# A hierarchical mixture-of-experts trunk on one core: half of the read-back by plain loads, placing matrices by GpSimd, weight rows in pairs, and a reordered passage to the experts

## What is computed

```python
h = rmsnorm(x, norm_ffn)                      # x is (512, 1024)
gl = h @ w_group + b_group                    # 4 groups
el = (h @ w_router + b_router)                # 16 experts, 4 in each group
g_idx = argmax(gl); top_v, top_i = top_k(el of that group, 2)
wts = softmax(top_v) * softmax(gl)[g_idx]
gate = sum over the two of one_hot(g_idx * 4 + top_i) * wts
for e in range(16):                           # EXPERT_FF = 512
    a = silu(h @ w_gate[e]) * (h @ w_up[e])
    out = out + gate[:, e:e + 1] * (a @ w_down[e])
x = x + out
return rmsnorm(x, norm_final)
```

## Time and profile before

| | |
|---|---|
| Median of 3 runs | 730.58 us (729.27 to 730.77) |
| The profiled execution, its own time | 730.31 us |
| Its span in the profile | 728.6 us |
| PE busy | 699.1 us (96%) |
| DVE busy | 518.7 us (71%) |
| ACT busy | 401.8 us (55%) |
| POOL busy | 128.5 us (18%) |
| TensorE clock granted, mean | 0.99 |

### The profile page before, as it was taken

The page is one execution under the profiler, slowest core; times in us unless marked ns, Lnnn a source line. Parts: engine busy times, 40 slices in busy tenths (PEclk is TensorE's granted clock), DMA queues, the critical chain, the costliest instruction groups (busy, mean ns, idle before and its releaser), DMA issues.

```text
span 728.6 us, 9970 instructions
## 1 busy us (share of the span) xinstructions
PE 699.1 (96%) x3557; PEld 582.1 (80%) x3557; DVE 518.7 (71%) x554; ACT 401.8 (55%) x407; POOL 128.5 (18%) x145
## 2 busy tenths in 40 slices
PE   5999999999999999999999989999999999999982
PEld 4898888888888888888889758888888888888861
DVE  4688776898526061441744678999999999999975
ACT  6626665666522131222403336877777777777742
POOL 5320000000000000000000150333333333333132
PEclk9999999999999999999999999999999999999997
DMA  9675330000232233223593379999999999999886
GB/s 327 165 263 180 116 97 20 29 13 4 94 124 80 92 101 121 95 87 113 177 363 126 130 269 393 395 390 369 372 365 379 373 369 371 373 368 372 316 159 188
DMA packets 86753, 159.15 MB, mean 218 GB/s; under 512 B 6274, under 2 KB 37116, under 8 KB 86724
## 3 DMA queue, kind: packets, MB, share of 16 engines
q1 hardware_dynamic: 78544, 137.38, 53.0%
q0 software_dynamic: 8128, 21.37, 9.3%
q10 hardware_dynamic: 52, 0.01, 0.0%
HBM read 150.64 MB, written 15.73 MB: 228 GB/s over the span
## 4 chain that ended last, share of the span: by engine, by line
PE 84%; DVE 5%; DMA 5%; ACT 3%; issue 1%; POOL 1%; POOLq 0%; SPq 0%; DVEq 0%; ACTq 0%
PE ps L519 24%; PE ps L521 24%; PE ps L520 24%; DMA x<-y_rows 3%; PE ps L1614 2%; DVE ring_lo L487 2%; PE ps L1540 1%; DMA xn<-in_x 1%; PE ps L1671 1%; PE ps L1568 1%; PE ps L1398 1%; DVE soft L1935 1%; PE ps L1360 1%; PE ps L1640 1%; ACT ring_hi L481 1%
## 5 line engine op out<-in xcount | busy, mean ns | idle before, releaser
L487 DVE TENSOR_TENSOR ring_lo<-raw_a,ring_hi 128x2048 fp32r<-128x2048 f32 (+2 forms) x58 | 115.5, 1995 | 96.7 <-ACT ring_hi L481 96.7
L487 DVE TENSOR_TENSOR ring_lo<-raw,ring_hi 128x2048 fp32r<-128x2048 f32 x71 | 161.3, 2290 | 11.1 <-ACT ring_hi L481 9.9
L481 ACT ACTIVATE ring_hi<-raw 128x2048 fp32r<-128x2048 f32 x71 | 136.2, 1920 | 19.3 <-PE ps L521 19.3
L481 ACT ACTIVATE ring_hi<-raw_a 128x2048 fp32r<-128x2048 f32 (+2 forms) x58 | 97.4, 1680 | 33.5 <-PE ps L521 30.6
L519 PE MATMUL ps<-hT_hi,ring_hi 128*128 128x512 f32 x288 | 113.4, 394 | 1.6 <-DVE hT_lo L1791 1.0
L521 PE MATMUL ps<-hT_hi,ring_lo 128*128 128x512 f32 x288 | 112.2, 390 | 0.0
L520 PE MATMUL ps<-hT_lo,ring_hi 128*128 128x512 f32 x288 | 112.2, 390 | 0.0
L519 PE MATMUL ps<-ring_hi,xT_hi 128*128 128x512 f32 x240 | 95.0, 396 | 1.8 <-DVE xT_lo L2173 1.7
L521 PE MATMUL ps<-ring_hi,xT_lo 128*128 128x512 f32 x240 | 93.8, 391 | 0.0
L520 PE MATMUL ps<-ring_lo,xT_hi 128*128 128x512 f32 x240 | 93.6, 390 | 0.0
L519 PEld LDWEIGHTS ps<-hT_hi,ring_hi 128*128 128x128 f32 x288 | 54.1, 188 | 13.0 <-DVE ring_lo L1786 1.2
(11 more groups left out here) (369 smaller groups left out, 1241.1 us busy)
## 6 DMA issues: line engine op xcount, KB each, us to landing
raw<-in_w_down SPq DMA_DIRECT2D x25, 1024.0 KB
raw<-in_w_gate SPq DMA_DIRECT2D x47, 512.0 KB
raw<-in_w_up SPq DMA_DIRECT2D x47, 512.0 KB
raw_a<-in_w_in SPq DMA_DIRECT2D x15, 1024.0 KB
raw_a<-in_w_gate SPq DMA_DIRECT2D x17, 512.0 KB
raw_a<-in_w_up SPq DMA_DIRECT2D x17, 512.0 KB
raw_a<-in_w_down SPq DMA_DIRECT2D x7, 1024.0 KB
raw_a<-in_w_in SPq DMA_DIRECT2D x10, 512.0 KB, 8.3
```

The lines of the kernel that those rows point to most:

```text
L481: act.activation(ring_hi[:, c[0] % SPLIT, 0:width], buf[:, 0:width], ACT.Copy).then_inc(hi_ready, 1)
L487: dve.tensor_tensor(ring_lo[:, s, 0:width], buf[:, 0:width], ring_hi[:, s, 0:width].bitcast(F32), ALU.subtract).then_inc(lo_ready, 1)
```

## The change

**Read-back.** The rows with r = 0 are now loaded by SP with four plain DMAs into `y_in`, a view of the first two buffers `raw_a`, when these chunks are split and the stores have landed; DVE adds them to `x2` (`add_rows`). POOL keeps the four adding DMAs with r = 1. DVE's order at the end becomes: low part of tile 14, `add_rows` 0 and 1, low part of tile 15, `add_rows` 2, `add_placed` 0 and 1, `add_rows` 3, `add_placed` 2 and 3.

**Places.** POOL writes `tok` and `place_l` for the last two tiles, behind its last store and ahead of the adding DMAs, once the chunk that lay in `place_l`'s memory is split.

**Pairs.** For experts 1 to 15 a chunk's partition p holds rows 2p and 2p + 1 (one run of 4 KB in HBM, 8 KB for `w_down`) in place of rows p and p + 128. PE's transposes take every second column accordingly (`pair_block`). Expert 0 keeps its loads.

**Passage.** Expert 0's product goes to banks 7 and 4 in place of 0 and 1; ACT alone copies `xT_f` (now in memory of its own) in four signalled pairs, and PE starts on the first pair; `rows_of_slots` moves ahead of block 3 and `x_transpose` of expert 1 ahead of the last block. DVE makes the picks (8 small operations) before the last ranks arrive, does `xT_lo` of expert 1 between the two splits, and the router's weights after the third. ACT splits the third chunk earlier. POOL's first gather takes its indices straight from `x_row`. SP no longer waits for `xe_in[1]`.

```diff
-    xT_f = sb("xT_f", [P, D], F32, "m", 32 * KB)
+    xT_f = sb("xT_f", [P, D], F32, "m", 44 * KB)
+    y_in = raw_a[:, :, :].rearrange("p s (h d) -> p (s h) d", d=D)
+    FIRST_BANK = (7, 4)
...
+            def paired(rows_ap):
+                return rows_ap.rearrange("(p k) n -> p (k n)", k=2).unsqueeze(1)
             def expert_in(c, i, e):
                 k0 = 2 * i * P
-                load(c, [((0, CW // 2, 2), w_gate[0, e, k0:k0 + 2 * P, :].rearrange("(k p) n -> p k n", p=P)),
-                         ((CW // 2, CW, 2), w_up[0, e, k0:k0 + 2 * P, :].rearrange("(k p) n -> p k n", p=P))])
+                load(c, [((0, CW // 2, 1), paired(w_gate[0, e, k0:k0 + 2 * P, :])),
+                         ((CW // 2, CW, 1), paired(w_up[0, e, k0:k0 + 2 * P, :]))])
...
                     if n == 0 and i == 1:
                         sp.wait_ge(route_ready, 1)
-                        sp.wait_ge(xe_in[1], 16)
...
+            sp.wait_ge(lo_ready, split_count(K(C_OVER - 11)))
+            for b in range(2):
+                sp.wait_ge(y_out[b], 16 * (NE // 2 - 1))
+                sp.sem_inc(sp_free, 1)
+            for t in range(TB):
+                sp.dma_start(y_in[:, t, :], rows_of(t, 0)).then_inc(y_load[t // 2], 16)
...
-            x_load(1, 1, None)
+            pool.sem_inc(x_col_set, 1)
+            pool.indirect_dma_start(xe[1][:, :], None, h2_rows[:, :],
+                                    bass.IndirectOffsetOnAxis(x_row[:, 1:2].bitcast(U32), 0),
+                                    bounds_check=S - 1, oob_is_err=False).then_inc(xe_in[1], 16)
...
             y_store(NE - 3, 1, NE // 2 - 1)
+            pool.wait_ge(lo_ready, split_count(K(C_OVER - 5)))
+            for b, tile in ((0, NE - 2), (1, NE - 1)):
+                done(pool.tensor_copy(tok[b][:, 0:1], x_row[:, tile:tile + 1]))
+                for t in range(1, TB):
+                    ins = pool.tensor_scalar(tok[b][:, t:t + 1], tok[b][:, 0:1], float(-P * t), None, ALU.add)
+                done(ins)
+                for t in range(TB):
+                    pool.tensor_scalar(place_l[b][:, t, :], slot_no_f[:, :], tok[b][:, t:t + 1], None,
+                                       ALU.is_equal).then_inc(place_set, 1)
             for b in range(2):
                 pool.wait_ge(y_out[b], 16 * (NE // 2 - 1))
                 pool.sem_inc(pool_free, 1)
-            for r in range(2):
-                for t in range(TB):
-                    if r == 1:
-                        pool.wait_ge(y_back[t], 16)
-                    pool.dma_start(x2[:, t, :], rows_of(t, r), accum_op=ALU.add).then_inc(y_back[t], 16)
+            for t in range(TB):
+                pool.dma_start(x2[:, t, :], rows_of(t, 1), accum_op=ALU.add).then_inc(y_back[t], 16)
...
-            for k in range(4):
-                ins = act.activation(xT_f[:, k * P:(k + 1) * P], bank(2)[:, k * P:(k + 1) * P], ACT.Copy,
+            for k in range(KD):
+                if k == 4:
+                    act.wait_ge(xe_ps, 2)
+                ins = act.activation(xT_f[:, k * P:(k + 1) * P], bank(2 + k // 4)[:, k % 4 * P:(k % 4 + 1) * P], ACT.Copy,
                                      scale=gains[:, 2 * KD + 2 + k:2 * KD + 3 + k])
-            ins.then_inc(xe_h, 2)
+                if k % 2:
+                    ins.then_inc(xe_h if k < 4 else xe_l, 1)
+            split_hi(act, K(C_MOE + DIRECT + 2))
...
+            def pair_block(rows_ap, k):
+                return rows_ap[:, 2 * P * (k // 2):2 * P * (k // 2 + 1)].rearrange("s (p k) -> s k p", k=2)[:, k % 2, :]
...
-                    ins = pe.transpose(bank(2, 2)[:, k * P:(k + 1) * P], xe[b][:, k * P:(k + 1) * P], ident[:, :])
+                    ins = pe.transpose(bank(2, 2)[:, k * P:(k + 1) * P], pair_block(xe[b], k), ident[:, :])
...
+                pe.wait_ge(xe_h if i < 2 else xe_l, i % 2 + 1)
                 for kk in range(2):
                     k = 2 * i + kk
+                    if k == 3:
+                        rows_of_slots()
+                    if k == KD - 1:
+                        x_transpose(2, 1, 1, 1)
...
-                        else:
-                            place_tile(0, NE - 2, 0)
-                            place_tile(1, NE - 1, 1)
+            def add_rows(t):
+                dve.wait_ge(y_load[t // 2], 32)
+                dve.wait_ge(y_back[t], 16)
+                dve.tensor_tensor(x2[:, t, :], x2[:, t, :], y_in[:, t, :], ALU.add).then_inc(y_added, 1)
+
             yl_low(0, 1, NE - 2)
+            add_rows(0)
+            add_rows(1)
             yl_low(1, 3, NE - 1, END_BANK)
+            add_rows(2)
```

More of the change, by code:

```diff
@@ L417, in build_trunk @@
         y_zero = sem("y_zero")
-        zero_set = sem("zero_set")
+        y_load = [sem(f"y_load{b}") for b in range(2)]
+        y_added = sem("y_added")
         wts_ready = sem("wts_ready")
-        w_split = sem("w_split")
         at_w_ready = sem("at_w_ready")
@@ L739, in _ @@
             pool.sem_inc(ye_free, 2)
-            pool.memset(zero_rows[:, :], 0.0).then_inc(zero_set, 1)
+            step(pool.memset(zero_rows[:, :], 0.0))
             inverse_root(slice(TB, TB + MB), TB + MB)
@@ L802, in _ @@
             pool.wait_ge(wts_ready, 1)
-            pool.tensor_copy(w_parts[:, :, 0], w_all).then_inc(w_split, 1)
-            pool.wait_ge(w_split, 1)
-            pool.tensor_tensor(w_rest[:, :], w_all, w_parts[:, :, 0], ALU.subtract).then_inc(w_split, 1)
-            pool.wait_ge(w_split, 2)
-            pool.tensor_copy(w_parts[:, :, 1], w_rest[:, :]).then_inc(w_split, 1)
-            pool.wait_ge(w_split, 3)
-            pool.tensor_tensor(w_parts[:, :, 2], w_rest[:, :], w_parts[:, :, 1], ALU.subtract).then_inc(w_split, 1)
-            pool.wait_ge(w_split, 4)
+            done = step
+            step(pool.tensor_copy(w_parts[:, :, 0], w_all))
+            step(pool.tensor_tensor(w_rest[:, :], w_all, w_parts[:, :, 0], ALU.subtract))
+            step(pool.tensor_copy(w_parts[:, :, 1], w_rest[:, :]))
+            step(pool.tensor_tensor(w_parts[:, :, 2], w_rest[:, :], w_parts[:, :, 1], ALU.subtract))
             pool.tensor_tensor(at_w[:, :, :, :],
@@ L1094, in xe_hi, with silu @@
                     act.activation(xT_hi[:, 512 * u:512 * u + 512], bank(2 + u), ACT.Copy).then_inc(xe_h, 1)
-            def silu(c):
+            def silu(c, b=0):
                 after(act, c)
-                act.activation(silu_g[:, :], bank(0), ACT.Silu).then_inc(silu_ready, 1)
+                act.activation(silu_g[:, :], bank(b), ACT.Silu).then_inc(silu_ready, 1)
             def aT_h(n, hi=aT_hi):
@@ L1639, in a_transpose @@
                 for f in range(4):
-                    ins = pe.transpose(bank(4)[:, f * P:(f + 1) * P], act_e[:, f * P:(f + 1) * P], ident[:, :])
+                    ins = pe.transpose(bank(4)[:, f * P:(f + 1) * P], pair_block(act_e, f), ident[:, :])
                 ins.then_inc(at_ps, 1)
@@ L2166, in _ @@
             choose(last, TB)
+            pick(m1, 0)
+            pick(m2, 1)
             place_last()
@@ L2288, in add_placed @@
                 ins.then_inc(sum_done, 1)
-            gated(1)
             xe_lo(2)
+            split_lo(dve, K(C_MOE + DIRECT + 1))
+            gated(1, FIRST_BANK[1])
             for i in range(PER_E):
                 split_lo(dve, K(C_MOE + 4 + i + 2))
+                if i == 0:
+                    dve.wait_ge(r_exp, 1)
+                    link(dve.tensor_reduce(sm[0][:, :], ex[:, :, 0:NG], AX_X, ALU.add))
+                    e2 = ex[:, :, 4:5].rearrange("p t o -> p (t o)")
+                    link(dve.tensor_scalar(sm[1][:, :], e2, 1.0, None, ALU.add))
+                    link(dve.tensor_tensor(sm[0][:, :], sm[0][:, :], sm[1][:, :], ALU.mult))
+                    link(dve.reciprocal(wts[:, 0, :], sm[0][:, :]))
+                    dve.tensor_tensor(wts[:, 1, :], wts[:, 0, :], e2, ALU.mult).then_inc(wts_ready, 1)
                 if i == 1:
```

52 lines of the change are left out of this document (19 added, 33 removed).

## The result

The changed kernel takes **739.13 us** (median of 4, 738.19 to 740.14) beside 730.61 for the kernel before: 1.0119 times as long, 95% interval 1.0105 to 1.0132. A repetition in another group of runs gave 1.0081 (1.0057 to 1.0104), and the two intervals don't overlap: the loss is 6.6 us by one group (738.25 less 731.70) and 8.5 by the other, so that differences of a us or two between groups say little. It is slower, and the time lies outside the range predicted. The profiled execution took 739.9, its span is 737.4 us.

The account below looks back on a forecast made before the run. PE was taken to bound the expert loop, and a read-back DMA the last addition; 730.31 - 1.6 (passage) + 1.3 (end) = 730.0 us, loop unchanged. The forecast's own range was 728.6 to 731.4, the overall range 725.0 to 732.8.

Parts of the forecast that it names:

- Expert 0's start, 0.5 us sooner: Passage: PE, waiting for two ACT copies instead of four, starts expert 0's product at some 414.4 instead of 414.92.
- The gather's issue at 420.8: Passage: with DVE's chain shorter and POOL's index copy gone, the gather is issued 3.4 us before the earlier 424.19.
- The landing after 6.6 us: Passage: the gather lands at 427.4, 6.6 us after issue, with 5.3 and 8.8 kept as ends.
- Wait 0.3, then two products in 1.7: Passage, PE: waits 0.3 us for the gather, transposes in 0.9, does two products in 1.7, starts `gate_up` at 430.0.
- Not all of it stays: After the passage: of 2.3 us gained at `gate_up`, only some 1.6 remain at expert 2's third chunk, as DVE hardly pauses.
- The stepped transposes at nothing: Expert loop, PE: the second column step of 12 transposes per expert costs nothing, since a two-float32 step keeps full bandwidth.
- its rival at 0.04: Expert loop: if the 140 ns weight load doubled and lay bare, 1.7 us in each of 15 experts: 755; chance 0.04.
- POOL held by the splits, one operation at a seam: End: POOL stands still during DVE splits, gets one operation through between two, and runs freely beside other DVE operations.
- A place at 0.20 to 0.24 us, at most 0.45: End, POOL: price of one of the 8 place operations, 0.20 to 0.24 us taken from a range of 0.19 to 0.45.
- T: End: the time at which POOL's adding DMAs start, forecast at 702.0 in place of 693.5.
- places at 0.45: End, rival: places cost 0.45 us each, fewer fit each window, T is 704.2 and the time 732.2; chance 0.12.
- 17.3 us from T to the last addition: End: second adding DMA lands after 8.8 us, then DVE's operations; the last addition starts at 719.3 against 718.04.

Follow-up runs that it names:

- passage alone: Changed kernel with places by DVE, weight rows as before, all eight adding DMAs by POOL, against the kernel before: 729.05 us, ratio 0.9971.
- pairs alone: Kernel before with weight rows of experts 1 to 15 in pairs and transposes with column step 2, nothing else: 732.15 us, ratio 1.0013.

## Why the prediction was wrong

The forecast was 730.0 us, with -1.6 for the passage, nothing for the loop and +1.3 for the end. What bounds the kernel and where POOL would be held were right. Four terms carry the miss: the gather's landing beside paired rows, the stepped transposes (put at nothing), the price of a place on POOL, and PE's products behind a long wait (also put at nothing). In the order of its steps:

- **Expert 0's start, 0.5 us sooner**: right. From the start of the last group of permuting products to that of expert 0's product it is 2.84 us in the profiles with the new passage and 3.36 in those with the old one. The 0.65 by which the profiled start (414.27) is sooner is partly the execution's course: the variants with the clock halved near 398 started at 414.7 to 416.0.
- **The gather's issue at 420.8**: 421.54. The removed copy and the wait behind it gave less than I took off. From the end of DVE's write of `x_row` (420.48) to the gather it is 1.06 us; before, it was 1.34 (422.85 and 424.19). The term of 0.98 was mis-sized, by 0.7.
- **The landing after 6.6 us**: 8.0, near the upper bound of 8.8. The passage alone shows 6.6, just as I took it, and -1.2 to -1.5 us: the passage's own working was nearly right. What failed is that I priced it apart from the pairs. From issue to PE's transposes it is 7.3 to 8.5 us in the five profiles with pairs and no wait of SP, 6.6 to 7.0 in the three with neither, and 6.5 to 6.8 in the three with the wait and the new gather, one of them with pairs. I had written that the longer runs spare the DMA queues work, and never asked what they do to the one transfer that is waited for. It is not the rate of the stream: from 424 to 428 it is 354 GB/s in the changed kernel and in the passage alone. What differs is the packets of SP's queue between 420 and 432, 4.3 KB on average (3.67 MB in 856) in place of 2.3 (3.65 MB in 1613); that the gather comes late because of their size is not shown. So PE waited 2.5 us, not 0.3: the transposes began at 429.53 in place of 427.4.
- **"Wait 0.3, then two products in 1.7"**: the four records took 3.55 at a granted clock of 0.50, and the eight transposes ahead of them stood at 0.9 in the sum where the earlier trace rows has 1.09. `gate_up` started at 433.26, not at 430.0.
- **"Not all of it stays", 0.7 us**: in the passage alone the loop got only 0.28 us longer (263.68).
- **The stepped transposes at nothing**: wrong, and its rival at 0.04 was too low. The weight load went from 140 to 209 ns, of which little lies bare: the loop is 263.68 to 263.72 us in the five kernels with the new passage and plain rows, and 265.35 to 265.38 in four with pairs. That is 1.65 us for the 14 experts of that stretch, 0.12 each. (The other 0.65 of the +2.31 in the ledger belong to the passage: the record of `gate_up`'s first product takes 1.15 there, 0.79 or 0.80 in the kernels with the new passage and the full clock, and 0.50 before, where PE had waited ahead of it.) The prediction drew on the Trainium skill (SBUF — State Buffer, "Door 1: The DMA port swizzle"), by which a step of two float32 still has full bandwidth. Here the trace differs: 69 ns more for a load of 128x128, and the measurement decides. The sign that I named, eight transposes longer than 1.09, came: 1.30, 1.23 in its variants, and 1.12 with the pairs alone.
- **POOL held by the splits, one operation at a seam**: right. Where DVE splits, POOL's operations take 2.2 to 2.5 us and end with the split (702.17 with 2.24, beside the split of 702.08 with 2.29). The Trainium skill (SBUF — State Buffer, "Who interferes with whom") said so, and the trace agrees.
- **A place at 0.20 to 0.24 us, at most 0.45**: this is the step that failed at the end. Free of any split the four places of the second tile take 2.37 us, **0.59 each**, and the shortest of all eight is 591 ns. I had taken the 128-element iota for the nearest row, an operation that reads nothing, and the upper bound from elements of a two-input operation of another shape. At 0.59 a window of 0.9 us lets one place through, not four or five. T is 707.49, in the time of before 707.49 - 3.27 = 704.2 in place of 702.0. The rival "places at 0.45" had 704.2 too: right in kind and place. That the number agrees is luck: it counted nine cheaper operations behind the last split, and there were seven dearer ones.
- **17.3 us from T to the last addition**: 19.7. The terms up to `add_rows` 1 hold (8.9 us after T against 8.8), but "PE's 24 products cost nothing more" doesn't: PE had idled 9.3 us behind DVE and did the first twelve at 1.2 GHz, and DVE waited 2.29 us for them.
- **The read-back by plain loads**: right in direction, 2.3 us of the end when the places don't stand ahead. The wait of 1.7 us for the last activations went as said, and with PE standing 9.3 us behind it, it was worth nothing here.

In one sum, in the time of the profile, the forecast is the start: 730.0, +4.9 up to the last transposes of `act_e` (+3.27 in place of -1.6), +2.2 for T, +2.4 for what follows it, -0.35 for the tail, +0.8 around the span (2.5 in place of 1.7) is 739.95, against 739.9. Of the 4.9, the gather has 2.1 (its later issue and its later landing), the transposes 0.2, the products at the halved clock 0.9, and what came behind the start of `gate_up` 1.6.

Open stays why the halved clock lies at 398 in one kernel and at 430 in another: it moved with PE's wait of 2.5 and 3.1 us for `xe`, but waits of 2.2 and 2.3 us did not bring it about there.

## What to carry to other kernels

An edit that moves work to an idle engine is priced by that engine's queue: what stands behind the moved work there, and who waits for it. Sixteen operations that DVE does in 2.5 us cost 8 to 10 on POOL, the larger part of it because four DMAs stood behind them. Take the price of an operation from a row with the same number of inputs from SBUF, or take the widest bound; and price parts together where one changes the packets beside which another's transfer runs.

## What the runs showed of the hardware

- A POOL operation with one input (128x128, float32 in, fp32r out, compare with a scalar per partition) takes 0.59 us when nothing holds it; DVE's takes 0.22 (0.87 for four).
- A float32 weight load for a transpose takes 140 ns with adjacent columns and 209 with every second one; 0.12 us per expert of 12 such transposes reaches the time.
- The first gather, beside the stream of weights, takes from its issue to PE's transposes 6.6 to 7.0 us with runs of 2 KB (4 KB for `w_down`), and 7.3 to 8.5 with runs twice as long, at the same 354 GB/s from 424 to 428 in one profile of each.
- Behind PE's waits of 9.2 to 9.8 us (four profiles) and of 3.5 us (one) its clock is at 0.50, and its products of 0.39 us take 0.63. In the passage the same came with waits of 2.5 and 3.1 us and not with those of 1.0 to 2.3. So a wait of PE can cost again behind its end: 2.29 us of DVE's time in the changed kernel.
